# One more matrix of an expert layer held outside the ring, its space taken from shared buffers

## The reference, cut to what matters

```python
for gi in range(MOE_GROUPS):                       # 4 groups of 4 experts
    hid = silu(einsum('td,edf->tef', t, w_gate[gi])) * einsum('td,edf->tef', t, w_up[gi])
    hid = hid * gate[:, gi, :, None]               # top group, top 2 experts in it
    y = y + einsum('tef,efd->td', hid, w_down[gi])
```

## Time and profile before

| | |
|---|---|
| median of 3 runs | 1030.85 us (1027.38, 1037.57, 1030.85) |
| profiled execution | 1031.11 us, of which the span from first to last instruction is 1029.3 us |
| granted TensorE clock over the span | 0.990 of full speed |
| busy: PE / PEld / DVE / ACT / POOL | 980.1 / 575.4 / 267.5 / 196.5 / 11.1 us |
| DMA | 282.50 MB, mean 274 GB/s |
| chain that ended last, by engine | PE 85%, DMA 10%, DVE 3%, issue 1%, SPq 1% |

### The profile page before, as it was taken

One profiled execution on the slowest core, in us unless ns is written; L12 is line 12 of the kernel. 1 busy time (PEld: TensorE's weight loads), 2 busy tenths in 40 slices (PEclk: granted clock), 3 DMA queues, 4 the chain that ended last, 5 costly groups with the idle time before them and its releaser, 6 DMA issues.

```text
span 1029.3 us, 10800 instructions
## 1 busy us (share of the span) xinstructions
PE 980.1 (95%) x4388; PEld 575.4 (56%) x4388; DVE 267.5 (26%) x655; ACT 196.5 (19%) x383; POOL 11.1 (1%) x21
## 2 busy tenths in 40 slices
PE   7999999999899998999999999999999898999995
PEld 5578468444243433488778877877475443434331
DVE  3334333331112111422202220221244311121115
ACT  3005312132111210301111110110122221212102
POOL 1110000000000000000000000000000000000000
PEclk9999999999999999999999999999999899999999
DMA  9793272369999989998193491688162699999993
GB/s 343 271 356 117 99 297 100 146 237 413 428 429 427 413 368 422 345 239 226 15 288 96 86 280 32 153 292 350 59 241 98 251 417 429 428 429 379 431 411 141
DMA packets 118484, 282.50 MB, mean 274 GB/s; under 512 B 4631, under 2 KB 82791, under 8 KB 107177
## 3 DMA queue, kind: packets, MB, share of 16 engines
q1 hardware_dynamic: 116992, 278.18, 74.0%
q0 software_dynamic: 1168, 3.40, 1.0%
q10 hardware_dynamic: 280, 0.31, 0.1%
HBM read 280.76 MB, written 1.11 MB: 274 GB/s over the span
## 4 chain that ended last, share of the span: by engine, by line
PE 85%; DMA 10%; DVE 3%; issue 1%; SPq 1%; ACT 0%; DVEq 0%
PE banks L1158 80%; DMA ring<-expert_w_up_in 6%; PE banks L1161 3%; DMA ring<-expert_w_down_in 3%; PE banks L1532 2%; SPq L613 1%; DMA scratch<-mem_in 1%; DVE h L1878 0%; ACT nrm L907 0%; DVE h L1870 0%; DVE mx L1994 0%; DVE nrm L1945 0%; DVE nrm L2002 0%; DVE late L759 0%; ACT late L757 0%
## 5 line engine op out<-in xcount | busy, mean ns | idle before, releaser
L1158 PE MATMUL banks<-ring,scratch 128*64 128x512 f32 (+1 forms) x1696 | 439.5, 597 | 19.6 <-DMA ring<-expert_w_up_in 9.8
L1158 PEld LDWEIGHTS banks<-ring,scratch 128*64 128x64 f32 (+1 forms) x1696 | 153.7, 145 | 268.3 <-issue 261.9
L1158 PE MATMUL banks<-late,ring 128*128 128x256 f32 x1040 | 227.2, 379 | 1.1 <-DVE late L759 0.6
L1158 PEld LDWEIGHTS banks<-late,ring 128*128 128x128 f32 x1040 | 196.5, 190 | 28.2 <-issue 1.9
L862 ACT ACTIVATE scratch<-banks 128x512 f32<-128x512 f32 (+4 forms) x100 | 66.7, 685 | 395.2 <-PE banks L1161 294.9
L1158 PE MATMUL banks<-ring,late 128*128 128x384 f32 (+2 forms) x320 | 102.7, 476 | 0.0
L2247 DVE TENSOR_SCALAR scratch<-banks 32x1024 f32<-32x1024 f32 x28 | 34.2, 1222 | 207.2 <-PE banks L1158 207.0
L1158 PEld LDWEIGHTS banks<-ring,late 128*128 128x128 f32 x320 | 57.4, 190 | 37.7 <-issue 7.7
L1158 PE MATMUL banks<-scratch 128*128 128x128 f32 (+5 forms) x388 | 78.1, 369 | 0.0
L1158 PEld LDWEIGHTS banks<-scratch 128*128 128x128 f32 (+2 forms) x388 | 48.5, 177 | 29.3 <-issue 21.5
L2225 DVE TENSOR_TENSOR scratch<-banks,scratch 128x512 f32<-128x512 f32 x16 | 16.9, 1058 | 120.3 <-PE banks L1158 120.3
(11 more groups left out here) (157 smaller groups left out, 439.6 us busy)
## 6 DMA issues: line engine op xcount, KB each, us to landing
ring<-expert_w_up_in SPq DMA_DIRECT2D x24, 2048.0 KB, 14.2
ring<-expert_w_gate_in SPq DMA_DIRECT2D x22, 2048.0 KB, 13.9
ring<-expert_w_down_in SPq DMA_DIRECT2D x20, 2048.0 KB, 13.1
ring<-odd_w_in_in SPq DMA_DIRECT2D x72, 512.0 KB, 7.3
ring<-expert_w_down_in SPq DMA_DIRECT2D x16, 1024.0 KB, 15.1
ring<-xkv_w_in SPq DMA_DIRECT2D x4, 2048.0 KB, 11.6
scratch<-expert_w_gate_in SPq DMA_DIRECT2D x4, 2048.0 KB, 12.7
ring<-expert_w_down_in SPq DMA_DIRECT2D x16, 512.0 KB, 8.0
```

The source lines that it names most:

```text
L1158: return giving_back(nc.tensor.matmul(dst, lhsT, rhs, start=start, stop=stop))
```

## The change

The ends of the edit: `FOURTH`, the first matrix of up 5, gets a place of its own in `scratch` and is loaded behind the third one, ahead of the layer's experts; the ring carries 44 instead of 45 matrices a layer. `scratch` grows by 1632 numbers a partition; the descriptor scratch of the DMAs that GpSimd issues shrinks from 8192 to 4096 bytes a partition. The rest of the 4096 numbers comes from sharing:

- `xg` has three halves of 128 columns per chunk; duo q's tokens stand in half q % 3. Where a group's two halves don't lie in a row (group 1: halves 2 and 0), its copies out of PSUM go in two instructions.
- `sel` holds two groups; the selectors of groups 2 and 3 are built behind the products of duos 1 and 3.
- SiLU writes into `hid`, in the product's order, and the product overwrites it in place; SiLU now waits for the flips of the duo before instead of the product.
- The router's small tiles lie in `ysb[:, 0]`, except `key` and `gates`.
- In the dilated layer the logits `op` and their flipped form `opT` lie in `nrm`.

```diff
-SCRATCH = 18176
+SCRATCH = 19808
...
-        op = a.take(2 * 512).rearrange("p (t k) -> p t k", t=2)
-        opT = a.take(2 * 512).rearrange("p (b q) -> p b q", b=2)
+        op, opT = (nrm[:, n].rearrange("p c q -> p (c q)").rearrange("p (t k) -> p t k", t=2) for n in range(2))
...
-        xg = a.take(2 * CH * EPG * SLOTS).rearrange("p (n c s) -> p n c s", n=2, c=CH)
+        xg = a.take(3 * CH * 2 * SLOTS).rearrange("p (c n s) -> p c n s", c=CH, n=3)
...
-        sel = a.take(TILES * EXPERTS * SHARE).rearrange("p (t s) -> p t s", t=TILES)
-        silu = a.take(FE)
+        sel = a.take(TILES * 2 * P).rearrange("p (n t s) -> p n t s", n=2, t=TILES)
         hid = a.take(FE).rearrange("p (c f) -> p c f", c=FC)
+        silu = hid
...
+        assert a.at <= SCRATCH - 3 * SLOT
+        fourth_slot, third_slot, spare_slot = (scratch[:, SCRATCH - n * SLOT:SCRATCH - (n - 1) * SLOT] for n in (3, 2, 1))
+        wa, wb = late_slot[:, :], spare_slot
+
+
+        spent = ysb[:, 0]
...
-            v = a.take(n)
+            v = passing(n)
...
+        FOURTH = PLACE["up", DUOS // 2 + 1]
+        HELD = {SPARE: (spare_slot, spare_in), LATE: (late_slot, late_in), THIRD: (third_slot, third_in),
+                FOURTH: (fourth_slot, fourth_in)}
...
                 else:
-                    sp.wait_ge(gate_ps, DUOS // 2 + 2)
+                    sp.wait_ge(up_ps, DUOS // 2 + 2)
                 sp.dma_start(spare_slot, rows_of(SPARE)).then_inc(spare_in, 16)
                 sp.dma_start(third_slot, rows_of(THIRD)).then_inc(third_in, 16)
+                sp.dma_start(fourth_slot, rows_of(FOURTH)).then_inc(fourth_in, 16)
...
+        def gathered_rows(g, c, src):
+
+            halves = [(2 * g + n) % 3 for n in range(2)]
+            if halves[0] < halves[1]:
+                runs = [(xg[:, c, halves[0]:halves[1] + 1, :].rearrange("p n s -> p (n s)"), tiles(src))]
+            else:
+                runs = [(xg[:, c, n, :], tiles(src)[:, :, 2 * i:2 * i + 2]) for i, n in enumerate(halves)]
+            return [(to.rearrange("p (e t s) -> p t e s", t=TILES, s=SHARE), rows) for to, rows in runs]
...
                     for i in range(2):
                         c = 2 * j + i
-                        last = nc.scalar.activation(by_tile(xg[:, g % 2, c, :]), tiles(pbank(k)[:, i * 256:(i + 1) * 256]),
-                                                    ACT.Copy, scale=gtok[:, l, c:c + 1])
+                        for dst, src in gathered_rows(g, c, pbank(k)[:, i * 256:(i + 1) * 256]):
+                            last = nc.scalar.activation(dst, src, ACT.Copy, scale=gtok[:, l, c:c + 1])
...
                     if x:
-                        act.wait_ge(hid_sb, x)
-                    nc.scalar.activation(silu, bank[0][:, :], ACT.Silu).then_inc(silu_sb, 1)
+                        act.wait_ge(hT_ps, x)
+                    nc.scalar.activation(silu.rearrange("p c f -> p f c"), bank[0].rearrange("p (f c) -> p f c", c=FC),
+                                         ACT.Silu).then_inc(silu_sb, 1)
...
-                    x = xg[:, (q // 2) % 2]
-                    at = P * (q % 2)
+                    x = xg[:, :, q % 3]
...
                 def selectors_of(g):
+                    if g >= 2:
+                        piece_in(dve, f"selT{l}{g - 2}")
...
                     v.tensor_tensor(hid.rearrange("p c f -> p f c"), bank[1].rearrange("p (f c) -> p f c", c=FC),
-                                    silu.rearrange("p (f c) -> p f c", c=FC), ALU.mult).then_inc(hid_sb, 1)
+                                    silu.rearrange("p c f -> p f c"), ALU.mult).then_inc(hid_sb, 1)
...
                     if q < DUOS - 1:
                         hidden(q)
+                    if half and g + 2 < GROUPS:
+                        selectors_of(g + 2)
...
-    nc = bacc.Bacc("TRN2", target_bir_lowering=False, num_devices=1, dynamic_dma_scratch_size=8192)
+    nc = bacc.Bacc("TRN2", target_bir_lowering=False, num_devices=1, dynamic_dma_scratch_size=4096)
```

More of the change, by code:

```diff
@@ L218, in encoder, with passing @@
         yrest = ysb[:, 1]
-        sel = a.take(TILES * EXPERTS * SHARE).rearrange("p (t s) -> p t s", t=TILES)
-        silu = a.take(FE)
+        sel = a.take(TILES * 2 * P).rearrange("p (n t s) -> p n t s", n=2, t=TILES)
         hid = a.take(FE).rearrange("p (c f) -> p c f", c=FC)
+        silu = hid
         hidT, last_hidT = (a.take(FE).rearrange("p (c s) -> p c s", c=FC) for _ in range(2))
         scat = a.take(TILES * P).rearrange("p (t q) -> p t q", t=TILES)
-        selr, gselr, scatr = (sel[:, 0, n * P:(n + 1) * P] for n in range(3))
+        selr, gselr, scatr = sel[:, 0, 0], sel[:, 0, 1], sel[:, 1, 0]
+        hidr, silur = (xg[:, FC * n:FC * (n + 1), 2, :] for n in range(2))
         kcur = a.take(TILES)
         gcur = a.take(TILES)
-        lg = a.take(TILES * NR).rearrange("p (t n) -> p t n", t=TILES)
+        key, gates = (a.take(TILES * EXPERTS).rearrange("p (t g e) -> p t g e", t=TILES, g=GROUPS) for _ in range(2))
+        assert a.at <= SCRATCH - 3 * SLOT
+        fourth_slot, third_slot, spare_slot = (scratch[:, SCRATCH - n * SLOT:SCRATCH - (n - 1) * SLOT] for n in (3, 2, 1))
+        wa, wb = late_slot[:, :], spare_slot
+        spent = ysb[:, 0]
+        taken = [0]
+        def passing(n):
+            taken[0] += n
+            assert taken[0] <= D
+            return spent[:, taken[0] - n:taken[0]]
         def small(*dims):
@@ L238, in small @@
             return v.rearrange("p (t g e) -> p t g e", t=TILES, g=dims[0])
+        lg = small(NR)
         gm, gsum, ggate, m1, m2, behind, ex2, w1, w2 = (small() for _ in range(9))
         gd, eg, oh = (small(4) for _ in range(3))
[L242 to L252, removed]
+        first, runner, spare, mask = (small(4, 4) for _ in range(4))
+        above = passing(TILES * 5 * 12)
+        rank = passing(TILES * 5 * 4)
+        most = passing(1)
         lnf = xkT[1].rearrange("p j m -> p (j m)")
@@ L1512, in gather @@
                             at = i * SEQ + t * P
-                            last = mm(pbank(k)[:, at:at + P], nrm[:, t, 2 * j + i, :], sel[:, t, P * g:P * (g + 1)], True, True)
+                            last = mm(pbank(k)[:, at:at + P], nrm[:, t, 2 * j + i, :], sel[:, g % 2, t], True, True)
                     last.then_inc(piece_ready, 1)
@@ L1520, in turned_selectors @@
                     for t in range(TILES):
-                        last = flip(pbank(k)[:, t * P:(t + 1) * P], sel[:, t, g * P:(g + 1) * P])
+                        last = flip(pbank(k)[:, t * P:(t + 1) * P], sel[:, g % 2, t])
                     last.then_inc(piece_ready, 1)
@@ L2202, in route @@
                         c = 2 * j + i
-                        last = v.tensor_scalar(by_tile(xg[:, 0, c, :]), tiles(pbank(k)[:, i * 256:(i + 1) * 256]),
-                                               gtok[:, l, c:c + 1], None, ALU.mult)
+                        for dst, src in gathered_rows(0, c, pbank(k)[:, i * 256:(i + 1) * 256]):
+                            last = v.tensor_scalar(dst, src, gtok[:, l, c:c + 1], None, ALU.mult)
                     last.then_inc(evac[k % 2], 1)
-                selectors_of(2)
-                selectors_of(3)
+                return selectors_of
             def experts(l):
-                route(l)
+                selectors_of = route(l)
                 def gate_selectors(g):
```

15 lines of the change are left out of this document (7 added, 8 removed).

## The result

| | before | changed |
|---|---|---|
| median of 12 runs on one chip | 1034.47 us (1027.38 to 1038.26) | 1028.47 us (1021.97 to 1033.03) |
| ratio, 95% interval | | 0.9945 (0.9923 to 0.9967) |
| profiled execution / its span | 1031.11 / 1029.3 us | 1021.97 / 1020.2 us |

The change makes the kernel faster by 0.55%, 5.7 us (3.4 to 8.0). The forecast was 1022.9 us; the profiled execution agrees with it to a microsecond and the median doesn't. That difference is half of what has to be explained.

A forecast was written before the change was run, and what follows sets the result against it. TensorE was busy almost everywhere, with expert waits on the weight stream behind up 5. Gains of 3.1 us (layer 0) and 4.9 (layer 1), all else nothing, sum to 8.0 off 1030.85: 1022.9 us, range 1018.5 to 1030.

The forecast's parts named there:

- The tenth place: Weight stream behind up 5: one 4.9 us transfer less per layer, gaining 3.1 us in layer 0 and 4.9 in layer 1.
- fetch gap: Middle of gate 7, layer 0: 1.88 us idle, taken for a late instruction fetch that comes again and limits the gain.
- Its cost where it goes: Ahead of each layer's experts: the moved load is hidden in a partly empty queue, cost nothing; uncovered, 4.9 us.
- The hole in the stream: Layer 1, 946 to 956 us: stream at 310 GB/s as a load waits for its slot; stays, one matrix later.
- SiLU and product: Expert activations in one buffer: SiLU 1.15 us, product 1.43 (between 1.06 and 2.04), both covered, nothing on the path.
- Split copies: ScalarE copies of gathered rows in group 1: four split ones cost 2.7 us, covered with 1.6 us to spare, nothing.
- selectors: VectorE: two instructions, 0.75 us for both, move behind the products of duos 1 and 3; nothing either way.
- descriptor scratch: GpSimd's DMA scratch halved: the sync engine's weight stream sees nothing, and router parameters still arrive in time.
- The tail's landings: Rival, last two duos: issue sets the landings, which don't move; little or no gain, 1029 to 1031 us, chance 0.20.
- product outlasted its cover: Slower rival: flips with 3.65 us of cover wait for the product; at 5.9 us it gives 1041 us; chance 0.07.
- both limits giving more: Rival, both layers' experts: fetch doesn't return or limits give more, 9.8 to 10.7 us, 1021.1 to 1020.2; chance 0.18.
- How the numbers follow: Closing part: chances (forecast 0.55), range, and 1%, 10.3 us, as about what measurement can tell from no change.

The follow-up runs named there:

- first pair: First profile of the kernel before and of the changed kernel, unaltered: experts' sum 417.55 and 408.52 us.
- experiments 2 to 4: Tenth place at up 3, changed kernel: 1.0012; third place at up 5, kernel before: 0.9969; third at up 2: before 0.9976, changed 0.9844 and 0.9866.
- experiment 1: The changed kernel without the tenth place, all shared buffers kept: 1034.15 us, ratio 0.9977 to the kernel before.
- early pairs: Profiles of both unaltered kernels whose layer 0 experts start at about 221 us: experts' sum 418.75 before, 408.77 changed.
- late profiles: Profiles of both unaltered kernels whose layer 0 experts start at about 228 us: experts' sum 416.99 before, 410.30 changed.

## Why the prediction was wrong

The mechanism and its sum held; the level they were set against and the conclusion drawn from them didn't.

- **The tenth place, 3.1 + 4.9 = 8.0 us.** Measured in the experts 3.7 + 5.3 in the first pair and 2.4 + 5.8 as a mean of both kernels' profiles, or, with the clock's stretches taken off, 3.2 + 4.9. So the 8.2 is no luck of two errors. The last landings moved by 5.1 and 5.3 us, forecast 4.9 each. The limits were right in both layers: layer 0 kept its fetch gap and had no weight wait behind it (TensorE's limit), layer 1 kept one wait of 0.92 us (forecast 0.9, the stream's limit). In layer 0 the last landing, at 422.28, stood 1.6 us ahead of its use at 423.9; forecast was 4.9 - 3.1 = 1.8. That TensorE is close behind was shown by taking one more transfer away.
- **Its cost where it goes**, forecast nothing: "between" is 377.62 in both first profiles.
- **The hole in the stream** stayed, 303 GB/s (310 before). I used it only to argue that the landings behind it move by one transfer. That it also decides which places are worth anything was in front of me and not drawn: experiments 2 to 4.
- **SiLU and product.** SiLU 1.07 us, forecast 1.15. The product 1.05, forecast 1.43: the lower bound was the value, a second operand read in steps costs nothing beside steps that are there already. The Trainium skill, "SBUF — State Buffer", section "Door 1: The DMA port swizzle", has each step to a new 16-byte line pay; VectorE's 1053 ns against 1058 don't agree with it here. ScalarE's output in steps does (1070 against 597).
- **Split copies** 2.18 us, forecast 2.7; **selectors**, **addresses**, **descriptor scratch**: no cost, shown together by experiment 1. The Trainium skill's statement that the sync engine's transfers never touch the descriptor rings in SBUF ("DMA: Bandwidth & Descriptors", section "SWDGE vs HWDGE vs iDMA") is borne out as far as half the scratch left the stream at 434 GB/s.
- **The rivals.** The tail's landings did move; no product outlasted its cover; both limits giving more (9.8 to 10.7) was met in number alone by the early pairs (10.0 us in the experts): its condition, a gap that doesn't come again, didn't hold.
- **Two readings were off**, and nothing rests on them: between slices 18 and 29 the DMA row goes down to one tenth, not zero, and 512 numbers in a row take 597 ns in the earlier trace rows, not 594.

**The step that failed is in "How the numbers follow": one per cent "is about what a measurement of this kernel can tell from no change".** I took it from three runs 10.2 us apart. Paired on one chip, twelve runs give an interval of 0.22 to 0.28% to each side, and before against itself gave 1.0006. A gain of 8.0 us, 0.8%, was by my own sum well outside that, so it could be told from no change; it was measured, at 0.55 and 0.67%.

**A second step was mis-sized: the profiled execution was taken as an ordinary one.** It lies 0.3 us above the median of three, so I took the sum off either. But it was of the early, shorter kind, and the medians lie nearer the late profiles' times. With twelve runs before's median is 1034.47: 3.6 of the 5.6 us between 1022.9 and 1028.47. The other 2.0 are gain that doesn't arrive. I let a half-clock stretch move a run "by 1.7 us either way", as noise alike for both kernels. It isn't alike: in late executions the changed kernel had 3.4 us more of it behind gate 7 in three profiles of three, 1.7 us, and 3.4 more in the router, some 0.8. In the late profiles the experts give 6.7 us; without that stretch it would be 8.4, and less both it is 5.9, by the comparisons' 5.7 and 6.9. Why the clock falls there, and what decides early or late, stays open; a variant that moves the gap without touching the stream wasn't tried.

## What to carry to other kernels

A prefetch place shortens only the stretch of the stream that its matrix leaves, up to the next point at which the ring runs full: find these holes first, and put one place into each stretch that ends in a wait. Before forecasting a gain under 1%, ask what a paired comparison can tell, not how far single runs scatter, and put the gain against a median and not against one profiled execution. When the stream's limit is moved, work out the next one: here TensorE's was reached in layer 0 after 3.1 of the 4.9 us, and lay 0.9 us off in layer 1.

## What was not expected of the hardware

- Behind the jump over the second pass's code TensorE stood idle for 1.83 to 2.21 us in layer 0, under "issue", in each of the 16 profiles that kept the code, with an instruction transfer of 16 KB and 1.02 us beside it; in neither of the two without the code, and not behind the same jump in layer 1.
- The clock is granted at half in different places for small shifts of the same work, and the same program has two kinds of start, 7 us apart: 3.3 us in the 33-row product (6.99 against 3.73 us), about as much in a stretch near 210.
- A product written in steps of 128 numbers takes 1053 ns whether its second operand is read in a row or in steps.
